# A two-layer decoder trunk on one core: in which order the expert weights are requested

## The reference, cut to what matters

```python
N_EXPERTS, TOP_K, EXPERT_DIM, D_MODEL, SEQ = 64, 8, 256, 1024, 512
scores = jax.nn.sigmoid(xt @ router_w)            # 512 x 64
_, eidx = lax.top_k(jnp.where(emask, biased, -jnp.inf), TOP_K)
gates = gates / jnp.sum(gates, -1, keepdims=True) * ROUTED_SCALE
def swiglu(x, w1, w3, w2):
    return (jax.nn.silu(x @ w1) * (x @ w3)) @ w2
def expert_block(acc, blk):                       # for every expert e
    y = swiglu(x_pad[tok], w1[e], w3[e], w2[e])
    return acc.at[tok].add(y * wt[:, None]), None
out = acc[:T] + swiglu(xt, ws1, ws3, ws2)
```

## Time and profile before

| | us |
|---|---|
| median of 3 runs | 2766.58 |
| lowest and highest | 2764.67, 2772.09 |
| the profiled execution: its time | 2764.67 |
| its span in the trace | 2763.1 |
| PE busy | 2539.0 (92%) |
| DVE busy | 1012.5 (37%) |
| ACT busy | 675.9 (24%) |
| POOL busy | 334.1 (12%) |
| DMA moved | 654.91 MB, mean 237 GB/s |

### The profile page before, as it was taken

One profiled execution on the slowest core, in us unless ns is written; L12 is line 12 of the kernel. 1 busy time (PEld: TensorE's weight loads), 2 busy tenths in 40 slices (PEclk: granted clock), 3 DMA queues, 4 the chain that ended last, 5 costly groups with the idle time before them and its releaser, 6 DMA issues. The chain is left out here.

```text
span 2763.1 us, 37355 instructions
## 1 busy us (share of the span) xinstructions
PE 2539.0 (92%) x13849; PEld 1388.1 (50%) x13850; DVE 1012.5 (37%) x2302; ACT 675.9 (24%) x1468; POOL 334.1 (12%) x390
## 2 busy tenths in 40 slices
PE   6999989899899999999986999999899999989995
PEld 3665646656674443333332576675784443333332
DVE  2443344433453322311216444454444322222216
ACT  1031030310312222222212333334312222222221
POOL 0101001010001111111100121121101111111110
PEclk9999999999999999999998999999899999999998
DMA  7624336152628899999964121211356999999966
GB/s 277 185 62 147 97 92 185 58 156 70 220 84 333 341 420 420 417 413 402 406 270 162 43 92 38 84 46 61 113 201 241 331 400 420 413 412 412 406 276 274
DMA packets 177812, 654.91 MB, mean 237 GB/s; under 512 B 26884, under 2 KB 88684, under 8 KB 122504
## 3 DMA queue, kind: packets, MB, share of 16 engines
q1 hardware_dynamic: 130320, 522.82, 48.3%
q0 software_dynamic: 35136, 109.10, 11.2%
q10 hardware_dynamic: 12216, 21.19, 2.7%
HBM read 614.18 MB, written 53.52 MB: 242 GB/s over the span
## 5 line engine op out<-in xcount | busy, mean ns | idle before, releaser
L1465 DVE TENSOR_SCALAR core_oT<-moe_tx,moe_by,moe_plus 128x128 f32<-128x128 f32 x360 | 123.0, 403 | 702.4 <-PE moe_tx L1712 702.2
L675 PE MATMUL attn_proj<-core_hT,core_ring 128*128 128x512 f32 x768 | 338.9, 602 | 8.6 <-issue 5.2
L1737 PE MATMUL moe_ph<-weights_w,core_oT 128*32 128x512 f32 (+2 forms) x1216 | 313.6, 628 | 22.4 <-issue 22.4
L1751 PE MATMUL moe_py<-weights_w,moe_hT 128*32 128x512 f32 (+2 forms) x1296 | 312.7, 596 | 1.0 <-ACT moe_hT L1192 0.9
L1737 PE MATMUL moe_pr<-weights_w,core_oT 128*64 128x512 f32 (+2 forms) x864 | 276.4, 604 | 7.4 <-issue 7.2
L675 PEld LDWEIGHTS attn_proj<-core_hT,core_ring 128*128 128x128 f32 x768 | 148.2, 193 | 191.8 <-issue 191.4
L2398 PE MATMUL gdn_pj<-core_hT,core_ring 128*128 128x512 f32 x512 | 226.6, 597 | 0.0
L1272 POOL DMA_INDIRECT y_rows<-moe_ysb,moe_yidx x90 | 92.3, 1025 | 959.8 <-ACT moe_ysb L1205 810.4
L1192 ACT COPY moe_hT<-moe_th 128x256 f32<-128x256 f32 x90 | 33.6, 374 | 660.1 <-PE moe_th L1700 660.1
L671 PE MATMUL attn_proj<-core_ring,core_hT 128*128 128x256 f32 x768 | 176.5, 391 | 0.0
L671 PEld LDWEIGHTS attn_proj<-core_ring,core_hT 128*128 128x128 f32 x768 | 169.3, 282 | 11.2 <-issue 3.8
(11 more groups left out here) (410 smaller groups left out, 3453.3 us busy)
## 6 DMA issues: line engine op xcount, KB each, us to landing
weights_w<-in_expert_w_dram SPq DMA_DIRECT2D x252, 1024.0 KB, 17.0
core_ring<-in_expert_w_dram SPq DMA_DIRECT2D x84, 1024.0 KB, 16.2
core_hT<-in_expert_w_dram SPq DMA_DIRECT2D x48, 1024.0 KB, 15.3
core_ring<-in_attn_w_in_dram SPq DMA_DIRECT2D x36, 1024.0 KB, 7.5
weights_w<-y_rows SPq DMA_DIRECT2D x32, 1024.0 KB, 12.9
attn_ada_w<-in_ada_w_dram POOLq DMA_DIRECT2D x64, 384.0 KB, 6.1
core_ring<-in_gdn_w_in_dram SPq DMA_DIRECT2D x16, 1024.0 KB, 6.0
attn_swp<-attn_raw ACTq DMA_DIRECT2D x192, 64.0 KB, 2.1
```

Of the source, the lines that this page charges most:

```text
L675: last = nc.tensor.matmul(proj[n % 2][:], w[:, j % SLOTS, kk, half_ * P:(half_ + 1) * P], c.hT[:, kk, :], start=kk == 0, stop=kk == KT - 1)
L1465: last = nc.vector.tensor_scalar(xT[:, b, k], tx[1][:, k - 4], by[:, k:k + 1], plus[:, k:k + 1], ALU.mult, ALU.add)
L1737: last = nc.tensor.matmul(ph[p % 2][at, :], xT[:, p % 2, k, at], w13[ew.up_place(n)[0]][:, :, k], start=k == 0, stop=k == KT - 1)
L1751: last = nc.tensor.matmul(py[n][at, :], hT2[:, p % 2, k, at], w2[ew.down_place(m)[0]][:, k, half(n)], start=k == 0, stop=k == 1)
```

## The change

The change is in what SP runs, and nowhere else. The list `down`, in which load n waited until three were in it, is gone; the loop now remembers one load. After load n's up transfers comes the down transfer of load n-1, where before came that of load n-2. The waits, slots, sizes and number of transfers are the same.

```diff
@@ -1079,15 +1079,14 @@
                     sp.wait_ge(y_done, last_pass[n - len(ew.DOWN_SLOTS)] + 1)
                 ew.load_down(sp, e, slot, w2_in[slot])
 
-            down = []
+            e_before = None
             for n in range(ew.EARLY, NE):
                 e = expert(n)
                 load_up(n, e)
-                down.append((n, e))
-                if len(down) == 3:
-                    load_down(*down.pop(0))
-            for n, e in down:
-                load_down(n, e)
+                if e_before is not None:
+                    load_down(n - 1, e_before)
+                e_before = e
+            load_down(NE - 1, e_before)
             sp.wait_ge(h_done, max(last_pass[n] for n in range(NE) if ew.up_place(n)[0] == 0) + 1)
             sp.dma_start(shared_down.rearrange("p k d -> p (k d)"), A["shared_w2"][l].rearrange("(p k) n -> p (k n)", k=2))\
```

## The result

The changed kernel takes 2789.03 us in the median (2785.49 to 2791.36, 4 runs) against 2766.33. The ratio is 1.0075, with a 95% interval from 1.0056 to 1.0092: 0.75% slower, some 21 us (15.5 to 25.5). The forecast was 18.8 us, and 2785.4.

A forecast was written before the change was run, and what follows sets the result against it. Transfers were taken to bound the expert loops once the engines are full. Later landings of up 59 than up 58, 9.5 + 9.3 = 18.8 us, gave 2783.5 us on the profiled execution, 2785.4 against the median; range 2771 to 2806.

The forecast's parts named there:

- The bound: In the expert loops, weight transfers bound passes 14 to 44: 13.5 us a pass against PE's 12.12.
- Two transfers late, one more ahead: At 951 two transfers fewer done, plus one more down ahead of each up: three transfers, 8.9 us.
- the third transfer: In SP's queue, one more down ahead of each up: 2.98 us later for each while the engines are full.
- Each up in the place of the next: From 951 on each load's ups take the next load's queue positions: 9.5 and 9.3 us for the two loops.
- The dry queue: After PE's waits SP's queue might run empty; nothing in the sum, up to 2 us at 8 waits a loop.
- rival B: Dry queue at down 21 and later downs behind PE's waits: up to 32 us more, 2815.5 us; chance 0.15.
- Waits and clock: PE's waits grow to about 35 us a loop; clock drop after the last wait, 3 us either way per loop.
- A: Idle engines in 877 to 951 absorb the lag: 2767 to 2773 us against the median; chance 0.17.
- C: Sooner requests fill idle engines in 834 to 951: faster, down to 2746.9 us; chance 0.05.
- D: Waits and not the order decide SP's issue times, so no effect; chance 0.03.

The follow-up runs named there:

- new_till21: The changed order for loads 3 to 21 only, the order of the kernel before from load 22 on: 2779.91 us, ratio 1.0059.
- dist0: Against the kernel before, load n's down transfer right behind its own up transfers, instead of load n-2's: 2979.06 us, ratio 1.0781.
- dist3: Against the kernel before, the down transfer of load n-3 behind load n's up transfers, instead of load n-2's: 2773.25 us, ratio 1.0034.
- new_from22: The order of the kernel before for loads 3 to 21, the changed order from load 22 on: 2772.68 us, ratio 1.0031.
- new_from44: The order of the kernel before for loads 3 to 43, the changed order from load 44 on: 2773.37 us, ratio 1.0033.

## Why the prediction was right, and where not

**The bound.** Right. Transfers bound the loops past the point where the engines fill up, and the slots and waits before it. PE's added time is 14.5 us of waits for up weights in the two loops, 8.9 us of products at the lower clock, and 2.4 us of waits for indices.

**Two transfers late, one more ahead.** Right in size. SP's queue in the early part of the first loop, before (834.43 to 951.2, when down 12 goes out) and after (835.65 to 954.5, the same point), packets, MB, share:

```profile
q1 hardware_dynamic: 4752, 34.61, 76.2%
```

```profile
q1 hardware_dynamic: 4464, 32.51, 71.7%
```

2.10 MB less, two transfers of 1.05 MB. Where they are lost is wider than I had it. I named the instant 951; but in the first 60 us of the loop alone the engines' share is 0.85 at 327 GB/s after and 0.94 at 366 before:

```profile
835.65:895.65 60.00, 1.00 0.85 327
```

```profile
834.43:894.43 60.00, 1.00 0.94 366
```

There too each up transfer stands behind one more down and its wait, and the decisive part is only that nothing makes it up later. With the third transfer, at the prediction's pace of 8.9 us for three, pass 16 would begin that much later; the mean over four loops is 9.0. New_till21 agrees: with the third given back, 2.1 of its 9.2 us come back, and 7.1 stay where two transfers are 6.0.

**Each up in the place of the next.** Right until pass 16, to some 2 us: up 20 was forecast at 1018.2 and pass 15 began at 1021.53, of which 1.2 us are the loop's later beginning and 2.1 came in the passes up to the 11th, which vary by 1 to 2 by themselves. The wait at pass 15 was forecast at 5.9 us and is 5.63. It holds less well further on. Pass 40 was forecast near 1365.7 and 2641, and began at 1369.20 and 2645.19. It was to begin 9.4 us late within its loop and began 12.4 us late in the mean (533.4 for 521.0 us from the loop's beginning).

**The dry queue, put at nothing.** This is the term that was mis-sized. The prediction put no dry queue into its sum and up to 16 us a loop at the end of its range. Between passes 16 and 40 the loops grew by another 3.4 us each, the difference of the table's middle column, so 7 of the 25.6 us of two loops, and the engines were idle there for 4.0 us more than before. The prediction's own sign for rival B, a falling share, came in small: 0.99 at 404 GB/s in the first loop, for 1.01 at 413. One place, after the wait at pass 15 (length, clock, share, GB/s), and the down transfer that SP issued into it at 1036.55:

```profile
1028.00:1032.00 4.00, 1.00 1.01 420
1032.00:1036.00 4.00, 1.00 0.88 369
1036.00:1040.00 4.00, 1.00 0.70 248
1044.00:1048.00 4.00, 1.00 1.03 426
```

```profile
1034.00:1035.00 1.00, 1.00 0.88 369
1035.00:1036.00 1.00, 1.00 0.72 303
1036.00:1037.00 1.00, 1.00 0.33 139
```

```profile
weights_w<-in_expert_w_dram SPq DMA_DIRECT2D x1, 1024.0 KB, 5.1
```

It is down 21, the place the rival named. It lands after 5.1 us, where those of the earlier trace rows took 16.8 to 25.6: there was next to nothing ahead of it. The prediction's count was right here. At PE's restart, 1021.53, six transfers were out (down 19, up 21, down 20, up 22), and the last of them landed at 1038.78, 17.3 us later. Its time for the next request was right too: 15.0 us after the restart, the 12.0 and 3.0 for the lower clock. The step that failed is the comparison of the two, which left a margin. A landing is later than the engines' work: down 21, with next to nothing ahead of it, took 5.1 us, where the pace is 2.98 us a transfer, so some 2 us of a landing are no work of the engines. And the engines don't end together: the rows have the share fall from 0.88 to 0.33 within two microseconds, and the sixteen notices that make up the landing of the last transfer came from 1035.51 to 1038.78. So the engines ran out while the last landing was still to come, and a request that leaves 2.2 us ahead of that landing finds them idle.

**Waits and clock.** PE's waits were to grow to about 35 us a loop and are 33.0 and 33.3; the 3.6 and 5.3 us of slower products that come with them were not forecast. In a loop that the transfers bound they need not add to the time, as PE would otherwise wait for as long, but no run here separates the two. A drop of the clock behind the last wait was there before and after (the product at 1369.20 takes 1.08 us), and it stayed a small term: from pass 40 to the end 67.2 us for 66.8.

**How close.** By the timed runs the forecast of 18.8 us lies within 15.5 to 25.5, with no dry queue in it. They can't show the missing term: it rests on the traced loops, 25.6 us in all, and on the engines' idle time in them.

**The rivals.** A, that the lag is absorbed, fell: nothing past pass 16 came back, except in new_till21 the transfer that the order itself gave back. B was true at a fifth of its upper price, 6.8 of 32 us. C fell with the traffic of the early part. D fell with the issue times.

## What to carry to other kernels

When transfers bound a loop, look for the moment at which the engines become full. Here what had not been requested by then was paid almost in full at the end, and from then on the order was a list of places. In a queue that issues in order, look for requests that could go and are held behind a wait that isn't their own: a hold of one pass cost 98 us a loop here. Count what is still out when the consumer resumes, and compare it with the time to the next request: allow for the two microseconds by which a landing is later than the engines' work. Here the order was worth some 10 to 13 us a loop with six transfers out, and about a hundred with three or four.

## What the runs showed that I had not expected

- The cost of shallow requests is a cliff. Down n-2, n-1, n behind up n: 587.8, 600.6, 695.8 us a loop. Holding the ups as long as dist0 does, in the order of before, gives 686.0.
- The balance of before is tight on both sides. One step further back (dist3) moves all 26 us of waits from the up products to the down products, 32.6 us, and none is gained.
- Stretches that the change does not touch vary by up to 4 us between executions (675.4 to 679.7 us between the loops, whatever the kernel), so a single span could not have told 3 us from 7. What stays open is how the 3.4, 6.6 and 3.6 us of after, new_from22 and new_from44 divide between the place in the queue and the dry places. The engines' idle time grew by 4.0, 5.2 and 4.3 us there, which is about all of it and leaves little for the transfer more ahead of each up. Whether new_from22 costs more than 3 to 5 us a loop at all, its timed runs leave open too.
